# The dilated heads' branch product as seven block products of two matmuls

## The reference

```python
h = rmsnorm(x, g_norm)
z = h @ w_in                                    # q, k, v and gates of all branches
y_a = (o_a * silu(dg)) @ w_br_diff              # differential heads, 1024 wide
y_b = (o_b * silu(lg)) @ w_br_dil               # dilated heads,      512 wide
y_m = (o_m * silu(mg)) @ w_br_mem               # memory heads,       512 wide
gates = sigmoid(mgate)                          # three gates of 1024 for each token
merged = gates[0] * y_a + gates[1] * y_b + gates[2] * y_m
x = x + merged @ w_out
```

## Time and profile before

| | us |
|---|---|
| median of three runs | 2078.49 |
| lowest and highest of them | 2075.92 and 2079.03 |
| the profiled execution | 2080.16 |
| its span, first to last instruction | 2078.3 |
| TensorE busy in it | 1822.0 (88%) |
| VectorE busy | 756.2 (36%) |
| ScalarE busy | 385.1 (19%) |

### The profile page before, as it was taken

How to read it: one execution, slowest core, us unless ns; L and a number is a source line. 1 busy time by engine, 2 the same in 40 slices (tenths; PEclk the granted TensorE clock), 3 DMA queues, 4 the chain that set the end, 5 groups by cost and what they waited for, 6 DMA issues and landing times.

```text
span 2078.3 us, 35046 instructions
## 1 busy us (share of the span) xinstructions
PE 1822.0 (88%) x15030; PEld 1208.6 (58%) x15030; DVE 756.2 (36%) x1288; ACT 385.1 (19%) x889; POOL 127.6 (6%) x186
## 2 busy tenths in 40 slices
PE   8998776777699877766769999999999999999998
PEld 4756455455557555554554588746554588746553
DVE  5651111111144111111105503473757503474656
ACT  4511011011022101100112112222221112222121
POOL 1200000000000000000001401200221001200000
PEclk9999988988899989889989999999999999999999
DMA  8599999999999999999998863443646563443331
GB/s 334 177 365 415 419 421 420 420 420 420 420 397 378 420 420 421 420 420 420 420 419 311 178 202 129 135 162 122 172 154 210 118 206 127 137 153 130 132 122 61
DMA packets 155639, 588.62 MB, mean 283 GB/s; under 512 B 16468, under 2 KB 34260, under 8 KB 106456
## 3 DMA queue, kind: packets, MB, share of 16 engines
q1 hardware_dynamic: 146936, 567.45, 70.9%
q0 software_dynamic: 8544, 18.89, 3.7%
HBM read 577.90 MB, written 8.39 MB: 282 GB/s over the span
## 4 chain that ended last, share of the span: by engine, by line
PE 62%; DMA 17%; SPq 12%; DVE 6%; issue 2%; ACT 1%; DVEq 0%; ACTq 0%
PE ps L640 17%; DMA ring<-in_moe_w_dram 16%; PE ps L607 15%; SPq L1397 8%; PE ps L1677 5%; SPq L1406 4%; PE ps L1657 3%; PE ps L1712 3%; PE ps L613 2%; PE ps L584 1%; PE ps L1968 1%; PE ps L617 1%; PE ps L523 1%; PE ps L557 1%; PE ps L1732 1%
## 5 line engine op out<-in xcount | busy, mean ns | idle before, releaser
L1677 PE MATMUL ps<-ring,xT 128*32 128x128 f32 x8192 | 302.8, 306 | 177.9 <-DMA ring<-in_moe_w_dram 171.9
L1677 PEld LDWEIGHTS ps<-ring,xT 128*32 128x32 f32 x8192 | 262.9, 121 | 243.7 <-DMA ring<-in_moe_w_dram 186.1
L607 PE MATMUL ps<-xT,ring 128*128 128x256 f32 x1408 | 310.1, 380 | 0.0
L607 PEld LDWEIGHTS ps<-xT,ring 128*128 128x128 f32 x1408 | 265.3, 190 | 39.7 <-issue 4.9
L2394 DVE TENSOR_TENSOR arena<-arena,ps 128x256 f32<-128x256 f32 x32 | 13.5, 421 | 558.3 <-ACT arena L2062 558.3
L1089 DVE TENSOR_TENSOR ring<-ring 128x2048 f32<-128x2048 f32 x64 | 146.7, 2292 | 15.6 <-PE ps L640 6.9
L640 PE MATMUL ps<-ring,xT 128*128 128x512 f32 x336 | 151.1, 594 | 0.5 <-ACT xT L774 0.5
L1712 PE MATMUL ps<-arena 128*32 128x512 f32 x768 | 120.1, 607 | 31.6 <-DVE arena L2394 31.6
L1330 POOL DMA_DIRECT2D ring<-gap_bias x160 | 96.4, 672 | 796.9 <-DMA ring<-in_w_in_dram 475.4
L1657 PE MATMUL ps<-arena,x_tm 128*128 128x128 f32 x1024 | 137.3, 291 | 0.0
L1657 PEld LDWEIGHTS ps<-arena,x_tm 128*128 128x128 f32 x1024 | 128.9, 205 | 10.8 <-issue 10.7
(11 more groups left out here) (316 smaller groups left out, 2003.0 us busy)
## 6 DMA issues: line engine op xcount, KB each, us to landing
ring<-in_moe_w_dram SPq DMA_DIRECT2D x287, 1024.0 KB, 26.1
arena<-in_moe_w_dram SPq DMA_DIRECT2D x89, 1024.0 KB, 26.8
ring<-in_w_in_dram SPq DMA_DIRECT2D x44, 2048.0 KB, 8.5
ring<-in_w_in_dram SPq DMA_DIRECT2D x16, 1024.0 KB, 12.1
ring<-in_w_br_diff_dram SPq DMA_DIRECT2D x4, 2048.0 KB, 10.5
ring<-in_w_out_dram SPq DMA_DIRECT2D x4, 2048.0 KB, 8.0
arena<-in_moe_w_dram SPq DMA_DIRECT2D x14, 512.0 KB, 15.6
ring<-in_w_mem_kv_dram SPq DMA_DIRECT2D x3, 2048.0 KB, 18.9
```

The costliest lines, as they stand in the source:

```text
L607: m = nc.tensor.matmul(bank[:, u * T:(u + 1) * T], w[:, k, f * P:(f + 1) * P], xT[:, k, :], start=(k == 0), stop=(k == KD - 1))
L1677: m = nc.tensor.matmul(ps[SL * q:SL * q + SL, g % 2, s * P:(s + 1) * P], xs[:, g % 2, k, s * SL:(s + 1) * SL], w[:, c0:c0 + 2 * P - 1:2], ...
```

## The change

The dilated branch alone goes over to the seven-product scheme. With the left operand's blocks a11, a12 (tokens 0 to 127, feature tiles 0 and 1, 2 and 3) and a21, a22 (tokens 128 to 255), and the weights' blocks b11, b12, b21, b22 (halves of the features by halves of the columns), each block product is two matmuls:

| unit | product | made from |
|---|---|---|
| 0 | a11 by b11 | |
| 1 | s4 by b22 | s4 = a12 - s2 |
| 2 | a12 by b21 | |
| 3 | s1 by first | s1 = a21 + a22, first = b12 - b11 |
| 4 | s2 by second | s2 = s1 - a11, second = b22 - first |
| 5 | a22 by fourth | fourth = b21 - second |
| 6 | s3 by third | s3 = a11 - a21, third = b22 - b12 |

TensorE goes through them as 0, 3, 2, then the head's transposes, then 4, 1, 6, 5. Units 0, 3, 2 and 1 go to banks 0 and 1 in turn, 4 and 6 share bank 3 and 5 has bank 4. ScalarE copies units 0 and 3 into SBUF; VectorE adds up the four output blocks and applies gates to them from SBUF. The sums s1 to s4 lie in the room of `mergedT`, first and second in that of the differential heads, third and fourth replace b12 and b21 in the slot. `br_begin` stands in the pair ahead, before the sum with that pair's last product. The memory branch stays in full. The rest of the diff is the counting of finished products (now seven for a chunk whose banks are taken four times).

```diff
+BR_UNITS = (0, 3, 2, 4, 1, 6, 5)
+BR_RING = (0, 3, 2, 1)
...
+            def br_product(l, i, u):
+                (a11, a12, _, a22), (s1, s2, s3, s4), (b11, b21, b12, b22), (first, second) = br_parts(i)
+                if u == 0:
+                    wait_chunk(pe, l, i)
+                    pe.wait_ge(sem("turn_read"), turns(l, BRANCHES[i]) + TILES[BRANCHES[i]] // 2)
+                if u in (3, 4, 6, 5):
+                    pe.wait_ge(sem("combined"), combined_for(l, (i, {3: "first", 4: "second", 6: "sum", 5: "fourth"}[u])))
+                if u < 4:
+                    n = AT[i, BR_RING.index(u)]
+                    pe.wait_ge(taken_of(l, n), products(l, n) // 2 + 1)
+                x_, w = ((a11, b11), (s4, b22), (a12, b21), (s1, first), (s2, second), (a22, b21), (s3, b12))[u]
+                for k in range(KH // 2):
+                    m = nc.tensor.matmul(ps[:, br_bank(l, i, u), :], x_[:, k, :], w[:, k, :],
+                                         start=(k == 0), stop=(k == KH // 2 - 1))
+                m.then_inc(sem("bank_full"), 1)
...
+            def br_copies(l, i):
+                first, _, third = br_sums
+                for half, dst in ((0, first), (1, third)):
+                    n = AT[i, half]
+                    act.wait_ge(sem("bank_full"), filled(l, n + 1))
+                    nc.scalar.copy(dst, ps[:, bank_at(l, n), :]).then_inc(taken_of(l, n), 1)
...
+                def br_begin(i):
+                    v.wait_ge(sem("turn_read"), turns(l, BRANCHES[i]) + TILES[BRANCHES[i]] // 2)
+                    (a11, a12, a21, a22), (s1, s2, s3, s4), (b11, _, b12, _), (first, _) = br_parts(i)
+                    ch(nc.vector.tensor_tensor(s1, a21, a22, ALU.add))
+                    ch(nc.vector.tensor_tensor(s2, s1, a11, ALU.subtract))
+                    ch(nc.vector.tensor_tensor(s3, a11, a21, ALU.subtract))
+                    ch(nc.vector.tensor_tensor(s4, a12, s2, ALU.subtract))
+                    combined()
+                    wait_chunk(v, l, i)
+                    ch(nc.vector.tensor_tensor(first, b12, b11, ALU.subtract))
+                    combined()
+
+                def br_second(i):
+                    _, _, (_, _, _, b22), (first, second) = br_parts(i)
+                    ch(nc.vector.tensor_tensor(second, b22, first, ALU.subtract))
+                    combined()
...
+                def br_rest(i):
+                    _, _, (_, b21, b12, b22), (_, second) = br_parts(i)
+                    first_sum, sum_, third = br_sums
+                    bank = lambda u: ps[:, br_bank(l, i, u), :]
+                    ch(nc.vector.tensor_tensor(b12, b22, b12, ALU.subtract))
+                    combined()
+                    wait_tanh(4)
+                    v.wait_ge(sem("bank_full"), br_filled(l, i, 2))
+                    wait_product_taken(v, l, AT[i, 0])
+                    ch(nc.vector.tensor_tensor(sum_, first_sum, bank(2), ALU.add))
+                    br_gate(0, 0, sum_)
+                    v.sem_inc(taken_of(l, AT[i, 2]), 1)
+                    ch(nc.vector.tensor_tensor(b21, b21, second, ALU.subtract))
+                    combined()
+                    v.wait_ge(sem("bank_full"), br_filled(l, i, 4))
+                    ch(nc.vector.tensor_tensor(sum_, first_sum, bank(4), ALU.add))
+                    combined()
+                    wait_product_taken(v, l, AT[i, 1])
+                    ch(nc.vector.tensor_tensor(first_sum, sum_, third, ALU.add))
+                    v.wait_ge(sem("bank_full"), br_filled(l, i, 1))
+                    ch(nc.vector.tensor_tensor(first_sum, first_sum, bank(1), ALU.add))
+                    br_gate(0, 1, first_sum)
...
```

More of the change, by code:

```diff
@@ L114 @@
     COMBOS += (["diff x"] if _i == DIFF_PAIR else []) + [(_i, j) for j in range(4)]
+    if _i + 2 in BRANCHES:
+        COMBOS += [(_i + 2, what) for what in ("x", "first", "second", "third", "fourth", "sum")]
 OUT_COMBOS = ["first w", "second w", "s1", "s2", "s4", "fourth w", "third w", "s3"]
@@ L512, in merged_combined, with br_parts @@
             return [b.rearrange("p (k t) -> p k t", k=KH) for b in (S1, S2, S3x)]
+        def br_parts(i):
+            x_, w = obT, cslots_wide[i % CRINGS]
+            half = KH // 2
+            x4 = [x_[:, k0:k0 + half, t0:t0 + P] for t0 in (0, P) for k0 in (0, half)]
+            w4 = [w[:, k0:k0 + half, c0:c0 + CW] for c0 in (0, CW) for k0 in (0, half)]
+            sums = [mergedT[:, j, :].rearrange("p (k t) -> p k t", k=half) for j in range(4)]
+            return x4, sums, w4, [w_first[:, k0:k0 + half, :] for k0 in (0, half)]
+        br_sums = S3[:, 2, :], S3[:, 1, :], PT3[:, 1, :]
         def pe_second(pe):
@@ L608, in product @@
                                                  start=(k == 0), stop=(k == KD - 1))
-                elif name in ("br_dil", "br_mem"):
-                    x_, w = (obT if name == "br_dil" else omT), cslots_wide[s]
+                elif name == "br_mem":
+                    x_, w = omT, cslots_wide[s]
                     t, cc = half // 2, half % 2
@@ L723, in pe_second @@
                         scores(l, *job, job_n)
-                    if chunk[0] == "br_dil":
-                        pe.wait_ge(sem("turn_read"), turns(l, "dil") + TILES["dil"] // 2)
-                    ahead = 2 if chunk[0] == "br_dil" else 1
-                    for half in range(ahead):
-                        product(l, i, half)
+                    if i in BRANCHES:
+                        for u in BR_UNITS[:3]:
+                            br_product(l, i, u)
+                    else:
+                        product(l, i, 0)
                     if job:
@@ L732, in pe_second @@
                         turn_after(l, after)
-                    for half in range(ahead, HALVES[i]):
-                        product(l, i, half)
+                    if i in BRANCHES:
+                        for u in BR_UNITS[3:]:
+                            br_product(l, i, u)
+                    else:
+                        for half in range(1, HALVES[i]):
+                            product(l, i, half)
                     if job:
@@ L901, in act_second @@
                         continue
+                    if i in BRANCHES:
+                        br_copies(l, i)
                     if job:
                         exps(l, *job, job_n)
-                    take(l, i, 0)
+                    if i not in BRANCHES:
+                        take(l, i, 0)
                     if job:
@@ L909, in act_second @@
                         take_after(after)
-                    for half in range(1, HALVES[i]):
+                    for half in range(1, 1 if i in BRANCHES else HALVES[i]):
                         take(l, i, half)
@@ L1149, in pair @@
                         diff_scales()
+                    if i + 2 in BRANCHES:
+                        br_begin(i + 2)
                     add_product(i, 6, first_part)
@@ L1304, in dve_second @@
                         scale_max(*job, job_n)
+                    if i in BRANCHES:
+                        br_second(i)
+                    if job:
                         weigh(*job, job_n)
@@ L1307, in dve_second @@
                         combine_x(chunk_of("br_diff", 0))
-                    for half in range(HALVES[i]):
-                        take(i, half)
-                        if chunk[0] == "br_mem" and half == 2:
-                            first_out_w()
+                    if i in BRANCHES:
+                        br_rest(i)
+                    else:
+                        for half in range(HALVES[i]):
+                            take(i, half)
+                            if chunk[0] == "br_mem" and half == 2:
+                                first_out_w()
                     if job:
```

39 lines of the change are left out of this document (32 added, 7 removed).

## The result

| | before | after |
|---|---|---|
| median, us (11 runs each) | 2078.49 | 2083.11 |
| lowest and highest | 2075.92, 2080.95 | 2079.74, 2084.55 |
| profiled execution, span | 2080.16, 2078.3 | 2082.76, 2080.7 |

The kernel became slower: ratio 1.0023, with an interval of 1.0014 to 1.0032, so +4.6 us (2.9 to 6.7), where +2.5 was forecast. The time lies within the predicted range and just past the 0.2% that a measurement can tell, a mark which lies inside its interval. Ratios and intervals are worked out over all runs, so they can differ in the fourth digit from the quotient of two medians. One run of the kernel before, of 6504.13 us, was a slow one and is left out of them.

What follows compares the result with a forecast made beforehand. TensorE, never idle around the branch, was taken as the bound. Per layer -1.72 + 0.54 + 2.45 = +1.27 us, +2.5 in two layers, on 2078.49 gives 2081.0 us; range 2077.2 to 2085.0.

Steps and rivals of the forecast that it cites:

- four records a layer saved: Dilated branch on TensorE: 16 matmuls become 14, saving 1.72 us a layer, 3.43 us in both.
- two waits added: TensorE in the branch: 0.54 us before the third product, 2.45 us before the sixth, in each layer.
- the rival with a fall in both layers: Clock falls behind the wait, 1.6 us a restart, 3.2 in two layers on top of +2.5: 2084.2; chance 0.05.
- signs named for being wrong: Sixth product waiting under 1.5 or over 3.5 us, next pair's transposes waiting, or granted clock under 1.00.
- a backlog in the next pair: Rival: slower VectorE gaps make the next pair's transposes wait too; +6.1 us, 2084.6; chance 0.15.
- a slowdown of over 0.2%: Measured time above 2082.7, from the backlog, the clock and a little of the main case; chance 0.22.
- the slack of 0.15 us: Next pair's transposes: their exponentials were to be ready some 0.15 us ahead, so no wait there.
- The first wait: Third product waits for ScalarE's copy of the first, queued behind two late tanh: 0.54 us a layer.
- VectorE's order and not its load decides: VectorE in the branch is busy 7.72 of 15.00 us; 1.225 us sums stand ahead of the awaited one.
- I place the new wait at the first row, at no cost: Sixth product's 2.45 us wait likened to a 2.67 us pause whose 64 matmuls took 2.03 us: no clock loss.
- The rule of the Trainium skill: TensorE pausing repeatedly while cycling PSUM banks switches clock levels; the branch would run partly at 1.2 GHz; set aside.

Runs made afterwards that it cites:

- weight sums early: Changed kernel with VectorE's third and fourth weight sums before any output sum, three gates late, early first copy, product and bank places moved; 2081.67 us, ratio 1.0017.
- gates split: As gates spread, but late gates' multiplications stay early, their adds follow the sum awaited by the pair's fifth product, next head's reciprocal later; 2074.59 us, ratio 0.9981.
- the run without the two sums: Changed kernel without the third and fourth weight sums on VectorE, the sixth and seventh products reading plain weights; 2076.21 us, ratio 0.9986.
- early copy: Changed kernel with ScalarE's copy of the first product ahead of the pair's last two tanh, into its own tile; 2082.36 us, ratio 1.0020.
- long pause: Kernel before, with TensorE waiting ahead of the branch's third quarter for VectorE's gate and an idle 128x896 sum; 2085.81 us, ratio 1.0036.
- own bank: Changed kernel with products 4 and 5 sharing bank 3 and the sixth product alone in bank 4; 2080.44 us, ratio 1.0009.
- gates spread: As weight sums early, but two of three late gates moved behind the sum that the next pair's fifth product awaits; 2077.63 us, ratio 0.9996.

## Why the prediction was right, and where it was not

The mechanism was right: four records a layer saved, two waits added, the longer behind a sum of VectorE. A term was too small, the clock's. The forecast of 2081.0 was 2.1 us low, and the rival with a fall in both layers, 2084.2, was 1.1 us high; one of the signs named for being wrong, a granted clock under 1.00, came true. That the time still lies in the range is luck in part, for the upper end was set by a backlog in the next pair, which didn't come; a slowdown of over 0.2% had only 0.22.

- *The saving*: 56 records as said, and 1.72 us a layer once nothing waits (weight sums early, gates split).
- *The two waits*: in the changed kernel's second layer, where the clock held, the sixth product began 11.88 us after the branch's start (chained 12.01, with both halves of the restart), the values came 1.23 late (1.27), the weighted head at 2007.78 was 20.01 behind the start (20.0), and the next transposes came 24.04 behind it, 1.24 later than before and without a wait, as the slack of 0.15 us allowed. The first wait was 0.40 us instead of 0.54. That VectorE's order and not its load decides was the step on which the forecast stood; the run with the gates split shows it, with the load unchanged, and the run without the two sums shows which of them stood in the way.
- *The clock* is the term that was mis-sized, and the step that failed is "I place the new wait at the first row, at no cost". I read one row of 2.67 us that held and gave a fall a chance of 0.05. The same trace has six pauses of 2.07 to 2.67 us in front of the same 64 small matmuls, and behind three of them the clock fell: at 736.95 (pause 2.07, then 3.42 for the 64), 767.23 (2.50, then 3.03) and 1040.15 (2.18, then 2.90). That one and one of equal length that held are shown below this list. So a chance of about a half could have been read before the run, and the runs showed the same: pauses of 2.29 to 2.46 us stood at ten places of the traces (changed kernel twice, early copy, long pause, weight sums early, two layers each), and behind six of them the clock fell, for 1.5 to 1.7 us each; behind pauses up to 1.50 us in these stretches it never did. The term was worth about a fall in every second place, and in the changed kernel one a run in both traces: 2 x 1.23 + 1.7 = 4.2, against the measured 4.6 (2.9 to 6.7). The size I had for a fall, 1.6 us from the earlier trace rows, was right.
- *The rule of the Trainium skill*: I cited the Trainium skill, TensorE: Matmul & The Clock Gate, section "A second HAM failure mode: psum-queue depth-cycling", and set it aside on that one row. Half of it came true: 1.2 GHz for some 3.4 us behind a pause, though behind single pauses of about 2.3 us, and in the kernel before as well. Whether the cycling through banks has a part in it no run here shows, since the kernel before, too, alternates between two banks.
- *Backlog into the next pair* did not occur in the changed kernel. It did in three variants that shortened or removed the pause with VectorE's work unchanged: as a wait for a bank (own bank, 1.00 us), for an output sum (weight sums early, 2.38) and for a weight sum (gates spread, 1.09). While TensorE pauses VectorE catches up; without the pause its queue has to be ordered one stage further.
- *A slip*: the range allows 0.4 us for the slowest run shown, which lay 0.5 over the median (2079.03 against 2078.49); nothing hangs on it.
- *Open*: what decides whether the clock falls behind a pause of this length. The layer, the kernel, and by the two rows of 2.18 us the length and the matmuls behind it don't, and nothing here was run to tell more.

The two pauses of 2.18 us in the trace of the kernel before:

```profile
526.97 2.03 PE L1677 MATMUL ps<-ring,xT 128*32 128x128 f32 x64 [2.18 <-DMA ring<-in_moe_w_dram]
...
1040.15 2.90 PE L1677 MATMUL ps<-ring,xT 128*32 128x128 f32 x64 [2.18 <-DMA ring<-in_moe_w_dram]
```

## What to carry to other kernels

Where TensorE is never idle, an operation that is traded for work on a half idle engine brings its full gain only if no awaited result stands behind that work; so chain the engine's queue with measured durations, up to the next awaited end, and again for the stage behind it, and reorder before giving up the trade. Split a step into the part that frees something (a bank, a tile, a weight) and the part that only adds up, and let the second wait. Count a TensorE pause of some 2.3 us at its length plus about half of what a fall of the clock costs (1.5 to 1.7 us here), and look up every pause of that length in the trace before taking one row that held as the rule.

## What the runs showed of the hardware that was not expected

- A pause of 2.3 to 2.5 us dropped the granted clock to 0.50 in six of ten occurrences, in identical kernels in one layer or the other; the 16 records behind it took 8.80 us instead of 7.10. In the kernel before, of two pauses of 2.18 us in front of the same 64 small matmuls, one dropped it (2.90 us) and one didn't (2.03).
- GpSimd doesn't run beside VectorE for nothing: its sum of 128x1024 took 2.35 us and held up VectorE's instructions between SBUF tiles (0.69 became 2.08), while those that read a PSUM bank kept 0.69.
